# Placing the last expert pair's rows from SBUF into the sums of the first token tiles, with their other rows reloaded during that pair

## The reference, cut to what matters

```python
h = h + short_conv_mixer(rmsnorm(h, ...), ...)        # layer 0
h = h + mla_mixer(rmsnorm(h, ...), ...)               # layer 1, 1024 tokens
# after either mixer:
h = h + hier_moe(rmsnorm(h, norm_ffn_g[i]), ...)
# in hier_moe, for each token, its two experts e with their gates:
y[token] += gate[token, e] * ((silu(x @ w_gate[e]) * (x @ w_up[e])) @ w_down[e])
return rmsnorm(h, final_norm_g)[:, 16:]
```

## Time and profile before

| | us |
|---|---|
| median of three executions | 2759.72 |
| the three executions | 2757.29, 2759.72, 2760.76 |
| span of the profiled execution | 2760.1 |

### The profile page before, as it was taken

The page is one execution under the profiler, slowest core; times in us unless marked ns, Lnnn a source line. Parts: engine busy times, 40 slices in busy tenths (PEclk is TensorE's granted clock), DMA queues, the critical chain, the costliest instruction groups (busy, mean ns, idle before and its releaser), DMA issues. The chain is left out here.

```text
span 2760.1 us, 39501 instructions
## 1 busy us (share of the span) xinstructions
PE 2466.4 (89%) x16330; PEld 1535.8 (56%) x16330; DVE 1066.0 (39%) x2180; ACT 541.8 (20%) x1226; POOL 342.3 (12%) x365
## 2 busy tenths in 40 slices
PE   9999988898999998987777899999999989777776
PEld 5444567547888655554444455766674555444443
DVE  3473654666555653211111154445545431111113
ACT  1312455210000011111111141322331111111112
POOL 3321002400000211111111100000003111111110
PEclk9999999999999999999999999999999999999998
DMA  3111010230113136999999970000113499999998
GB/s 118 35 38 53 5 48 5 79 114 34 43 46 119 71 135 246 420 424 425 425 425 426 405 304 24 17 25 8 52 45 137 159 401 425 425 425 426 425 424 341
DMA packets 88726, 566.06 MB, mean 205 GB/s; under 512 B 19408, under 2 KB 19568, under 8 KB 59344
## 3 DMA queue, kind: packets, MB, share of 16 engines
q1 hardware_dynamic: 63504, 506.86, 45.1%
q0 software_dynamic: 20144, 38.79, 3.7%
q10 hardware_dynamic: 4896, 17.83, 1.6%
HBM read 529.06 MB, written 65.01 MB: 215 GB/s over the span
## 5 line engine op out<-in xcount | busy, mean ns | idle before, releaser
L3249 PE MATMUL ex__h_ps<-all__arena,ex__xT 128*64 128x256 f32 x3392 | 406.8, 395 | 108.1 <-DMA all__arena<-in_w_up_t 84.0
L3249 PEld LDWEIGHTS ex__h_ps<-all__arena,ex__xT 128*64 128x64 f32 x3392 | 249.7, 142 | 277.2 <-DMA all__arena<-in_w_up_t 123.3
L3300 DVE COPY ex__ysb<-ex__y_ps 128x512 f32<-128x512 f32 x64 | 44.3, 692 | 493.0 <-PE ex__y_ps L3269 483.0
L3269 PE MATMUL ex__y_ps<-b__w,ex__hT 128*64 128x512 f32 x640 | 146.8, 600 | 27.7 <-issue 27.7
L3429 POOL DMA_INDIRECT b__rows<-s_hn,mo__queue x60 | 60.6, 1010 | 746.0 <-PE ex__x_ps L3242 746.0
L3291 DVE TENSOR_TENSOR ex__hs<-ex__sg,ex__h_ps 128x256 f32<-128x256 f32 x64 | 27.0, 421 | 305.4 <-PE ex__h_ps L3249 305.4
L2534 PE MATMUL cm__acc<-all__arena,cw__w 128*128 128x260 f32 x576 | 136.0, 386 | 2.6 <-PEq L84 2.3
L2534 PE MATMUL cm__acc<-all__arena,cm__sums 128*128 128x260 f32 x576 | 134.3, 383 | 0.0
L2534 PEld LDWEIGHTS cm__acc<-all__arena,cw__w 128*128 128x128 f32 x576 | 110.4, 192 | 20.4 <-issue 3.3
L2534 PEld LDWEIGHTS cm__acc<-all__arena,cm__sums 128*128 128x128 f32 x576 | 109.5, 190 | 17.2 <-issue 0.3
L3282 ACT COPY ex__xT<-ex__x_ps 128x512 f32<-128x512 f32 x64 | 37.4, 585 | 381.0 <-PE ex__x_ps L3242 381.0
(11 more groups left out here) (550 smaller groups left out, 4111.2 us busy)
## 6 DMA issues: line engine op xcount, KB each, us to landing
all__arena<-in_w_up_t SPq DMA_DIRECT2D x62, 2048.0 KB, 44.1
all__arena<-in_w_gate_t SPq DMA_DIRECT2D x40, 2048.0 KB, 43.2
b__w<-in_w_down_t SPq DMA_DIRECT2D x40, 2048.0 KB, 44.6
mo__wx<-in_w_gate_t SPq DMA_DIRECT2D x22, 2048.0 KB, 44.0
all__arena<-in_w_down_t SPq DMA_DIRECT2D x22, 1024.0 KB, 38.8
mo__wx<-in_w_down_t SPq DMA_DIRECT2D x20, 1024.0 KB, 44.2
all__arena<-s_ys SPq DMA_DIRECT2D x15, 1024.0 KB, 11.3
cw__w<-in_conv_w_in_t SPq DMA_DIRECT2D x24, 512.0 KB, 4.5
```

The costliest lines, as they stand in the source:

```text
L3249: last = nc.tensor.matmul(h_ps[half, c, DE * b:DE * b + DE], xT[:, b, k, half], slots[c][:, n, k], start=(k == 0), stop=(k == KT - 1))
L3269: last = nc.tensor.matmul(y_ps[half, c], hT[:, b, k, half], rows[k][:, n, 512 * c:512 * c + 512], start=(k == 0), stop=(k == 1))
L3300: return nc.vector.tensor_copy(ysb[:, b, 512:], y_ps[:, 1])
```

## The change

- **Early reload.** SP issues the reload of the first token tiles' rows (`EARLY`: tile 0 in layer 0, tiles 0 to 3 in layer 1) as soon as pair 30's scatter has landed. These reloads do not hold the last pair's rows.
- **Placement.** The last pair's rows stay in SBUF too (`last_rows`), and PE adds them to the early tiles' sums by a product with a matrix that puts each row at its token, times its gate (`places_of_last` writes it during pair 3, PE transposes it in pair 4). The gates for the reloaded rows are set to 0 where a token's row belongs to the last pair (`own_gate`).
- **Order of waits.** POOL waits, ahead of the last scatter, for the early tiles' reloads. The last scatter has a semaphore of its own (`last_stored`), and SP waits for it at the start of the next stage, where it then loads the rows of the other tiles.
- **Layer 0.** Tile 0's sum is made inside the `experts` stage: DVE makes the gated sum ahead of its half of the last pair's result copy, PE makes two placement products after it, DVE adds them. `scale_first` moves on ACT from the end of the stage to the last pair, between `silu` and `hT_copy`. `scale_second` moves from DVE to POOL in the next stage. The load of `wk` and residual tiles 1 and 2 go behind the early reload. The filler products fall from eight to one.
- **Layer 1.** The final norm's gains and residual tiles 4 to 7 are loaded behind the early reloads. Fillers fall from eight to four. In `combine_out` PE makes placement products for tiles 0 to 3; it now also sums tile 3, and DVE adds the placed rows to tiles 0 and 1.
- **First block.** POOL writes zeros over the first 128 tokens of `ys` with eight DMAs of 128 KB, and waits for them, in the window attention's stage.

```diff
                 pool.wait_ge(staged, 1 + TL)
+                zeros = ck.z[:].rearrange("p t a b -> p (t a b)")
+                n = TL * 2 * HALF
+                for at in range(0, 2 * DM, n):
+                    pool.dma_start(D["ys"][0:P, at:at + n], zeros).then_inc(rows_cleared, 16)
+                pool.wait_ge(rows_cleared, 16 * (2 * DM // n))
...
                 sp.wait_ge(m["h_done"], LAST_OF_RING + 1)
                 after.start(sp)
+                sp.wait_ge(m["h_done"], PAIRS_M - 1)
+                for b in range(2):
+                    sp.wait_ge(y_stored[b], 16 * (PAIRS_M // 2 - b))
+                for t in after.EARLY:
+                    after.rows_in(sp, t)
+                after.behind_early(sp)
                 with sp.If(0 < count):
                     sp.wait_ge(m["y_done"], PAIRS_M)
+                    for t in after.EARLY:
+                        sp.wait_ge(after.y_loaded[t], 16)
+                    if after.sums_here:
+                        sp.wait_ge(early_done, 2 * NE)
...
-                for b in range(2):
-                    sp.wait_ge(y_stored[b], 16 * (PAIRS_M // 2))
-                after.rows(sp)
+                    sp.wait_ge(after.last_stored, 16)
+                    for t in after.EARLY:
+                        after.rows_in(sp, t, again)
+                    sp.wait_ge(again, 16 * NE)
...
                 def scatter(p):
+                    landed = after.last_stored if p == PAIRS_M - 1 else y_stored[p % 2]
...
                 for p in range(PAIRS_M - 2, PAIRS_M):
                     pool.wait_ge(m["y_out"], 2 * (p + 1))
+                    if p == PAIRS_M - 1:
+                        for t in after.EARLY:
+                            pool.wait_ge(after.y_loaded[t], 16)
                     scatter(p)
                     if p < PAIRS_M - 1:
                         pool.drain()
                 for b in range(2):
-                    pool.wait_ge(y_stored[b], 16 * (PAIRS_M // 2))
+                    pool.wait_ge(y_stored[b], 16 * (PAIRS_M // 2 - b))
...
+                    if p == 5:
+                        pe.wait_ge(placed_out, 1)
                     turn_hidden(p % 2).then_inc(m["h_turned"], 1)
+                    if p == 4:
+                        pe.wait_ge(placed, 1)
+                        for t in range(NE):
+                            last = nc.tensor.transpose(turned_place(t), place[:, t], ident[:])
+                        last.then_inc(placed_turned, 1)
...
                     pe.wait_ge(d_ends[k], 16)
                     last = down_half((PAIRS_M - 1) % 2, d_slots[(PAIRS_M - 1) % RING].rows, k)
                 last.then_inc(m["y_done"], 1)
-                for n in range(8):
+                for n in range(after.FILL):
                     nc.tensor.matmul(x_ps[:, n % 2], ident[:], xe[:, 0, 0:512], start=True, stop=True)
+                if after.sums_here:
+                    pe.wait_ge(m["y_out"], 2 * PAIRS_M)
+                    pe.wait_ge(placed_out, 1)
+                    for c in range(2):
+                        nc.tensor.matmul(h_ps[:, c], place_t[:, 0], last_rows[:, 512 * c:512 * c + 512], start=True, stop=True
+                                         ).then_inc(early_product, 1)
...
                         y_half(p - 1)
+                    if end:
+                        after.scale_first(nc, act)
                     if p + 1 < PAIRS_M:
                         rows_out(p + 1)
                     act.wait_ge(m["h_turned"], p + 1)
...
-                            y_first(0).then_inc(s["y_out"], 1)
-                after.scale_first(nc, act)
...
+                    if p == 3:
+                        places_of_last(dve, v)
+                    if p == 4:
+                        dve.wait_ge(placed_turned, 1)
+                        for t in range(NE):
+                            v.hold(nc.vector.tensor_copy(place_t[:, t], turned_place(t)))
+                        v.wait()
+                        dve.sem_inc(placed_out, 1)
...
+                if after.sums_here:
+                    dve.wait_ge(after.h_loaded[0], 16)
+                    dve.wait_ge(after.y_loaded[0], 16)
+                    gathered_sum(nc, v, after.yb[:, 0], own_gate, after.hb[:, 0], after.ho[:, 0], 0)
                 y_half(PAIRS_M - 1)
+                if after.sums_here:
+                    for c in range(2):
+                        part_of = slice(512 * c, 512 * c + 512)
+                        dve.wait_ge(early_product, c + 1)
+                        v.hold(nc.vector.tensor_tensor(after.ho[:, 0, part_of], h_ps[:, c], after.ho[:, 0, part_of], ALU.add))
+                    v.wait()
+                    dve.sem_inc(early_done, 2)
...
+    EARLY = (0,)
+    FILL = 1
+    sums_here = True
+    early_gate = early_place = last_rows = None
...
+    def behind_early(self, sp):
+        D = self.D
+        sp.dma_start(self.wk[:], D["w_dkv_t"]).then_inc(self.wk_loaded, 16)
+        for t in range(1, self.NBUF):
+            self.residual_in(sp, t)
         sp.dma_start(self.gq[:], D["cq_g_t"]).then_inc(self.gl_loaded, 16)
         sp.dma_start(self.gk[:], D["ckv_g_t"]).then_inc(self.gl_loaded, 16)
-        sp.dma_start(self.wk[:], D["w_dkv_t"]).then_inc(self.wk_loaded, 16)
...
+    def scale_second(self, nc, pool):
+        pool.wait_ge(self.g_loaded, 32)
+        pool.wait_ge(self.wk_loaded, 16)
         for k in range(KT):
-            nc.vector.tensor_scalar(self.wk[:, k], self.wk[:, k], self.gains[:, 1, k:k + 1], None,
+            nc.gpsimd.tensor_scalar(self.wk[:, k], self.wk[:, k], self.gains[:, 1, k:k + 1], None,
                                     ALU.mult).then_inc(self.k_scaled, 1)
...
+                sp.wait_ge(pre.last_stored, 16)
+                for t in range(len(pre.EARLY), NBUF):
+                    pre.rows_in(sp, t)
...
                 make_identity(nc, pool, ident, const_done)
                 nc.gpsimd.memset(eps[:], NORM_EPS).then_inc(const_done, 1)
+                pre.scale_second(nc, pool)
                 for t in range(TT):
                     pool.wait_ge(made, t + 1)
                     pool.dma_start(h_out[P * t:P * t + P], ho[:, t % NOUT]).then_inc(stored[t % NOUT], 16)
...
-                make(0)
+                dve.sem_inc(made, 1)
                 scale(0)
...
+    EARLY = (0, 1, 2, 3)
+    FILL = 4
+    sums_here = False
...
-        self.gb = part(8, DM)
+        self.gb = gb
+        self.last_rows = part(8, DM)
+        self.early_place = spare.rearrange("p k g -> p (k g)")[:, 0:P * len(self.EARLY)]
+        self.early_gate = ph.sb("early_gate", [P, len(self.EARLY), 2])
+        self.last_stored = ph.sem("final_last_stored")
...
     def start(self, sp):
+        for t in self.EARLY:
+            self.residual_in(sp, t)
+    def behind_early(self, sp):
         sp.dma_start(self.gb[:], self.D["final_norm_g_2"].partition_broadcast(P)).then_inc(self.g_loaded, 16)
-        for t in range(self.TT):
+        for t in range(len(self.EARLY), self.TT):
             self.residual_in(sp, t)
...
+        BY_PE = (2, 3, 4, 6)
+        TURNS = (0, 1, 2, 3, 5, 4, 7, 6)
+        MADE = (0, 1, 5, 7)
+        ADDED = (0, 1)
+        last_rows, early_gate = pre.last_rows, pre.early_gate
+        early_place = pre.early_place.rearrange("p (t s) -> p t s", t=len(EARLY))
...
+        bank_of = {0: 0, 1: 1, 2: 2, 3: 3, 4: 0, 6: 1}
...
+                sp.wait_ge(pre.last_stored, 16)
                 for t in range(NBUF, TT):
                     sp.dma_start(yb[t], D["ys"][P * t:P * t + P]).then_inc(y_loaded[t], 16)
...
+                def place_last(t, alone):
+                    for c, part_of in halves:
+                        last = mm(acc[:, bank_of[t], c], early_place[:, t], last_rows[:, part_of], start=True, stop=alone)
+                    if alone:
+                        last.then_inc(placed, 1)
+                def sum_rows(n):
+                    t = BY_PE[n]
+                    if n == 0:
+                        pe.wait_ge(const_done, 3)
                     pe.wait_ge(h_loaded[t], 16)
+                    if t not in EARLY:
+                        pe.wait_ge(added, bank_of[t] + 1)
+                    for c, part_of in halves:
+                        mm(acc[:, bank_of[t], c], ident[:], hb[:, t, part_of], start=(t not in EARLY), stop=False)
                     pe.wait_ge(spread_done, 2 * (n + 1))
                     pe.wait_ge(y_loaded[t], 16)
-                    for c in range(2):
-                        part_of = slice(512 * c, 512 * c + 512)
-                        nc.tensor.matmul(acc[:, n, c], ident[:], hb[:, t, part_of], start=True, stop=False)
+                    for c, part_of in halves:
                         for e in range(2):
-                            last = nc.tensor.matmul(acc[:, n, c], spread[:, n, e], yb[t][:, DM * e + 512 * c:DM * e + 512 * c + 512],
-                                                    start=False, stop=(e == 1))
```

(33 more changed lines are left out.)

109 lines of the change are left out of this document (64 added, 45 removed).

## The result

| | before | after |
|---|---|---|
| median of four executions, us | 2760.09 | 2781.72 |
| the executions, us | 2757.29 to 2760.76 | 2779.75 to 2784.65 |
| span of the profiled execution, us | 2760.1 | 2779.5 |

The ratio is 1.0082, with a 95% interval of 1.0068 to 1.0096: the change costs 21.6 us, where the prediction had 3. Both joints got longer.

The account below looks back on a forecast made before the run. It took the scatter-and-reload waits at both joints as what the change could save. Layer 0 +4.8 (8.65 + 2.85 - 7.0 + 0.3) and layer 1 -1.5 made span 2763.4, time 2763.0 us; range 2755 to 2769.

Parts of the forecast that it names:

- a slow scatter: Rival, layer 1: the last scatter lands after 14.7 us instead of 7.5, +6.0 on the forecast, 2769 us; chance 0.22.
- `scale_first` (+8.65): Layer 0, last pair: ACT waits for `wq` until 1586.8, then scales, so `hT_copy` starts 8.65 us later.
- ACT's wait is small: Rival, layer 0: `wq` lands by 1578, the layer is worth 0, time 2758.2 us; chance 0.15.
- Down products at the low clock (+2.85): Layer 0, last pair: after PE's idle time the down products take 6.5 us instead of 3.65, +2.85.
- DVE's early sum under ACT's wait (0): Layer 0: tile 0's sum ahead of DVE's copy ends at 1593.2, under the down products' 1598.0, costing nothing.
- What the early reload saves in layer 0 (-7.0): Layer 0, copied result to tile 0's transposes: 8.4 us instead of 15.5, a saving of 7.0.
- Pair 30's scatter, the early reloads, POOL's wait in layer 1 (+10): Layer 1: the last early reload lands at 2726.1, so POOL issues the last scatter 10 us late.
- Layer 1 gains 5: Rival, layer 1: even DMA engines let DVE start 5.3 us sooner, gain 5, time 2759.5 us; chance 0.17.
- Its sums start about 1 us (issue) and 1.6 us (change of stage) later: Layer 1: `combine_out`'s sums on DVE start at 2728.8, after the last scatter is held until 2726.1.
- DVE is the bound: Layer 1, `combine_out`: DVE sets the end, last scaling at 2754.0 instead of 2755.5, -1.5 us.
- From span to time (-0.4): Whole program: the span stands 0.4 us over the median, so span 2763.4 gives time 2763.0 us.
- No cost for zero writes and placement preparation: `experts` and earlier stages: zero writes fit POOL's free 77 us, placement work hides behind a 44 us queue; cost 0.

Follow-up runs that it names:

- `scale_first` back: Kernel after, with ACT's `scale_first` moved back to the end of layer 0's `experts` stage, behind its half of the last result copy: 2776.57 us.
- the scatter apart in layer 0: Layer 1 as before; layer 0 with `scale_first` back, DVE's sum behind its copy, nine fillers; its last scatter to an unread tensor, without POOL's wait: 2763.60 us.
- the fillers' versions above: Layer 1 as before, layer 0 with `scale_first` back, DVE's sum behind its copy, nine fillers: 2765.04 us; kernel after with 20 fillers in layer 1: 2782.82 us.
- the profile with two early tiles: Layer 1's part alone, with two early tiles instead of four, tile 3 on DVE, tile 2 a plain sum on PE: 2762.72 us.
- the scatter apart in layer 1: Kernel after, with layer 1's last scatter to a tensor that nobody reads and POOL not waiting for the early reloads: 2773.96 us.

## Why the prediction was wrong, step by step

It had 2763.0 us; measured were 2781.72. The 18.7 us are 1.6 in layer 0, 13.9 in layer 1, 0.6 elsewhere, and 2.6 in the step from span to time. No rival reached that: the highest, a slow scatter, had 2769. Of the signs that the prediction names, those of layer 0 were seen (`scale_first` at 1586.2, `hT_copy` at 1590.3, the low clock, the transposes at 1608.4 for 1607); in layer 1 DVE was not gapless, it waits 4.1 us ahead of its scaling at 2758.

- **`scale_first` (+8.65): right.** `w_dq` landed after 29.5 us as forecast, `hT_copy` stands 9.19 us after the turned rows against 0.54, which is 8.65. "ACT's wait is small" fell; and the move alone costs the kernel before 10.6 us (2771.62 against its 2761.06 beside it).
- **Down products at the low clock (+2.85): right in kind.** They took 4.98 in this profile, +1.3, and as much with tile 3 by DVE. In the four other profiles in which ACT's wait stands they took 6.03 to 6.54, against the forecast's 6.5. Executions of the same code differ in when the clock falls and rises.
- **DVE's early sum under ACT's wait (0): right.** It ended at 1592.6, and bound as soon as ACT's wait was gone.
- **What the early reload saves in layer 0 (-7.0): wrong, it is 3.6** (2.4 to 3.8 over the five profiles with this code). From copied result to transposes it took 11.86, not 8.4. The step that failed is "the change of stage and POOL's identity, 2.0": the stage begins only once the last scatter has landed, 4.6 us after its issue, and PE's warming starts 6.2 us after the copy where the sum had 4.2. The other 1.5 are the warming products, 5.83 (up to 7.11 in the others) instead of 4.1: before, they ran beside DVE's work on tile 0, now they stand in the way, and the forecast took them at the full clock. `scale_second` took 10.49 instead of 7.1, and was covered.
- **Tile 1's wait (+0.3): right, it is nothing.** Its transposes start 7.4 us after tile 0's, against 7.5 before.
- **Pair 30's scatter, the early reloads, POOL's wait in layer 1 (+10): right.** The reloads leave 8.1 us after that scatter and the last lands 16.8 us later (2733.2), against 17.2. POOL is 11.0 late, as it issues the scatter only 0.9 us after that landing. "Layer 1 gains 5" (even engines) fell with it.
- **"Its sums start about 1 us (issue) and 1.6 us (change of stage) later": wrong, and worth 4.7.** I took it that the stage ends when the scatter is issued, and that only SP's reloads 4 to 7 wait for its landing. The scatter landed 6.1 us after 2734.11, at 2740.2, and the stage began at 2741.39. DVE's first sum stands 7.4 us behind the scatter's issue and not 2.7, and 19.2 behind the copy and not 13.6 (the other 1.0 is the item above). So the scatter was not slow, as the rival on the other side had it (it needed 10 us); its ordinary landing was in the way, and with four early tiles it stands there in full. With the scatter sooner, the way was 9.9 us shorter.
- **"DVE is the bound": wrong, and worth 8.2.** The forecast costs DVE's work item by item and gives PE's products no sum, only the words that tile 2 is ready by then. The placement products of 9.91 and four tiles of 5.15 are 30.5 us without a gap, and a square, a root and a scaling stand behind them: DVE's last scaling ends 33.4 us after its first sum, not 25.2. Each product of 512 columns stands in the rows as two records of 0.43 us: 8 placement products are x16, a tile's six are x12. Before, PE had three tiles in the same place. Moving a tile to DVE gave 2.5 back, with DVE bound from there: its last scaling then ends 6.1 us after PE's last product.
- **From span to time (-0.4): wrong by 2.6.** I compared the span of one profiled execution to the median of others. All twelve executions profiled since have their own time 1.7 to 2.1 us above their own span. By that the one profiled before took about 2761.8, more than any of the four that are listed (an estimate; its own time is not listed).
- **No cost for zero writes and placement preparation: right as far as seen.** The kernel after reaches layer 0's joint at 1581.08, before at 1581.80, and the middle part of the span is 1.4 us longer, within what it varies by. No version leaves these parts out alone.

The windows show what I take to be behind it. Of 8 us behind the last scatter DMA is idle for some 5, before (0.59 and 0.22 of it busy from 2716 to 2724) and after (0.28 and 0.41 from 2736 to 2744). The change was to close that hole and moved it instead: the loads that used to fill the time before the scatter now stand ahead of the scatter itself.

## What to carry to other kernels

An early load whose source is written once more later turns the later write into a waiter: price what hangs on that write, with its landing, before what the load saves. Where work is moved from the bounding engine to a free one, sum up that engine's stage as well, in records of the trace and not in products of the source. When one wait hides others, taking it back returns little: only the version with that wait alone shows its price. And look in the trace for what a version waits for last: nine fillers as long as the wait that was taken out hid what its removal gives.

## What the hardware showed that was not expected

- **A stage whose last POOL instruction is an indirect DMA ends when it has landed.** In the kernel after no instruction of the program that runs in the `experts` stage waits for the last scatter (only spilled branches do). Yet the next stage's first instruction came 1.3 and 1.2 us after its landing (layers 0 and 1), and 1.2 to 1.3 us in every other version with this order of waits but two, for landings from 3.2 to 8.3 us after the issue. In those two another engine ended its stage later: 2.0 with `scale_first` back (DVE's second addition ended at 1595.4, after the landing at 1594.9) and 2.1 with the scatter apart in layer 0 (the fillers). What waits is a DRAIN on POOL at the end of the block, from 2734.4 to 2740.3, with the landing at 2740.21 (the block's line, 2720 to 2745: shortest/median/longest in ns, and first and last start):

```profile
L3429 POOLq DRAIN  x1: 5880/5880/5880, 2734.4 to 2734.4; - x1
```

- **PE's clock fell after pauses of 1.93 and 2.79 us** (the fillers' versions above: 1.00 in the window in which PE resumed, 0.50 in the next), while it stayed up after a pause of 1.91 us with the scatter apart in layer 0 (warming products of 4.14). Before, after a pause of 3.05 us, they took 4.14; with the same code and a pause of 3.06 us, in the profile with two early tiles, they took 5.83:

```profile
1596.68 5.83 PE L3968 MATMUL cl__aq<-all__arena 128*128 128x384 f32 x12 [3.06 <-POOL cl__eps L3888]
```

  So it is not the length of the pause alone; what tells them apart no run here shows. There it cost nothing (way 20.8), as DVE's work for tile 0 was as long.
- **POOL's multiplication of 128x320 took between 1.08 and 2.03 us.** In `scale_second` the two longest, 2.03 and 1.49, are those that ran beside DVE's two sums of 1.28 and 1.43 at 1606.95 and 1608.27; four others took 1.08 to 1.10, and two, beside DVE's reciprocal and scaling, 1.37 and 1.40. The Trainium skill (SBUF — State Buffer, SBUF: two separate sides) has an exclusive lock on the shared port pair for a whole instruction in just that pairing; the trace agrees in kind, with 1.4 us added over both of the longest; it does not settle that the lock is exclusive, as 1.4 us is about half of the two sums.
- **A scatter beside a backlog is not held by it.** In the version with the scatter apart in layer 1 it landed 8.3 us after its issue, at 2737.9, ahead of the residual tiles that SP had issued up to 4.6 us before it and that took a median of 19.4. The Trainium skill (DMA: Bandwidth & Descriptors, Queues, rings and completion order) says that an engine takes turns between queues packet by packet; the trace agrees.
